# Head norms' sums of squares in two split passes, with the opening's loads and the store of x reordered

## The reference

```python
mod = silu(c) @ w_ada + b_ada                       # shift1, scale1, gate1, shift2, scale2, gate2
h = rms_norm(x, norm1_w) * (1 + scale1) + shift1
q_a, k_a, v_a, q_f, k_f, v_f, f_logit, g_a, g_f = split(h @ w_in)
q_a, k_a = rope(rms_norm(q_a, swa_q_norm_w)), rope(rms_norm(k_a, swa_k_norm_w))   # per head of 128
q_f, k_f = rms_norm(q_f, fox_q_norm_w), rms_norm(k_f, fox_k_norm_w)               # per head of 128
merged = sigmoid(g_a) * (window_attention @ w_o_swa) + sigmoid(g_f) * (forgetting_attention @ w_o_fox)
x = x + gate1 * (merged @ w_out)
x = x + gate2 * (silu(g) * u) @ w_ffn_out           # g, u from a second adaLN norm of x
```

## Time and profile before

| | |
|---|---|
| median of 3 runs | 2699.12 us (2698.11 to 2699.68) |
| profiled execution, its own time | 2696.75 us |
| span of the profiled execution | 2695.1 us |
| TensorE busy | 2637.9 us, 98% of the span |
| VectorE busy | 1970.2 us, 73% |
| ScalarE busy | 1034.2 us, 38% |
| mean transfer rate | 181 GB/s |

### The profile page before, as it was taken

One profiled execution on the slowest core, in us unless ns is written; L12 is line 12 of the kernel. 1 busy time (PEld: TensorE's weight loads), 2 busy tenths in 40 slices (PEclk: granted clock), 3 DMA queues, 4 the chain that ended last, 5 costly groups with the idle time before them and its releaser, 6 DMA issues.

```text
span 2695.1 us, 44512 instructions
## 1 busy us (share of the span) xinstructions
PE 2637.9 (98%) x17066; PEld 2397.4 (89%) x17066; DVE 1970.2 (73%) x3066; ACT 1034.2 (38%) x1402; POOL 298.8 (11%) x290
## 2 busy tenths in 40 slices
PE   5899999999999999999999999999999999999999
PEld 5678888878888888888899999999999999999998
DVE  6888877743333357755568888888888888888886
ACT  4332333333433322222354444444444444333343
POOL 0033223210001011122100000000000000010100
PEclk8999999999999999999999999999999999999999
DMA  9986666533333277777434444544544559595753
GB/s 334 294 256 181 179 187 173 148 100 94 102 94 102 71 226 242 235 233 233 151 94 157 158 136 157 160 137 154 163 136 151 165 203 339 166 347 177 262 214 120
DMA packets 399485, 487.17 MB, mean 181 GB/s; under 512 B 19029, under 2 KB 338793, under 8 KB 398793
## 3 DMA queue, kind: packets, MB, share of 16 engines
q1 hardware_dynamic: 364296, 353.12, 42.1%
q0 software_dynamic: 32896, 127.28, 13.5%
q10 hardware_dynamic: 2112, 4.19, 0.4%
HBM read 414.80 MB, written 69.73 MB: 180 GB/s over the span
## 4 chain that ended last, share of the span: by engine, by line
PE 91%; DMA 4%; DVE 2%; SPq 1%; issue 1%; ACT 1%; DVEq 0%; POOL 0%; ACTq 0%; POOLq 0%
PE bank L913 15%; PE bank L916 15%; PE bank L915 15%; PE bank L592 12%; PE bank L594 12%; PE bank L593 12%; DMA ramp_w<-in_w_ada 3%; PE bank L743 1%; PE bank L721 1%; PE bank L768 1%; SPq L482 1%; PE bank L732 1%; PE bank L862 1%; PE bank L866 1%; PE bank L864 1%
## 5 line engine op out<-in xcount | busy, mean ns | idle before, releaser
L913 PE MATMUL bank<-mov,w_slot 128*128 128x256 f32 x3472 | 983.6, 283 | 0.9 <-ACT blocks L1201 0.9
L916 PE MATMUL bank<-mov,w_slot 128*128 128x256 f32 x3472 | 982.6, 283 | 0.0
L915 PE MATMUL bank<-mov,w_slot 128*128 128x256 f32 x3472 | 982.5, 283 | 0.0
L913 PEld LDWEIGHTS bank<-mov,w_slot 128*128 128x128 f32 x3472 | 666.5, 192 | 1.1 <-ACT blocks L1201 1.1
L915 PEld LDWEIGHTS bank<-mov,w_slot 128*128 128x128 f32 x3472 | 666.6, 192 | 0.0
L916 PEld LDWEIGHTS bank<-mov,w_slot 128*128 128x128 f32 x3472 | 666.5, 192 | 0.0
L1289 DVE TENSOR_TENSOR w_lo<-w_raw,w_hi 128x1024 fp32r<-128x1024 f32 x192 | 241.8, 1260 | 377.7 <-ACT w_hi L943 377.0
L592 PE MATMUL bank<-h_hi,w_hi 128*128 128x512 f32 x1280 | 509.4, 398 | 0.0
L594 PE MATMUL bank<-h_hi,w_lo 128*128 128x512 f32 x1280 | 499.3, 390 | 0.0
L593 PE MATMUL bank<-h_lo,w_hi 128*128 128x512 f32 x1280 | 498.4, 389 | 0.0
L1140 ACT ACTIVATE w_slot<-w_raw 128x768 fp32r<-128x768 f32 x248 | 209.8, 846 | 557.7 <-PE bank L916 553.1
(11 more groups left out here) (241 smaller groups left out, 2784.1 us busy)
## 6 DMA issues: line engine op xcount, KB each, us to landing
w_raw<-in_w_ffn_in SPq DMA_DIRECT2D x352, 256.0 KB, 3.1
w_raw<-in_w_ada SPq DMA_DIRECT2D x128, 512.0 KB
w_raw<-in_w_ffn_out SPq DMA_DIRECT2D x88, 512.0 KB, 5.7
u_fm<-u_stage POOLq DMA_DIRECT2D x22, 1792.0 KB, 8.4
mov<-u_fm POOLq DMA_DIRECT2D x22, 1792.0 KB, 21.3
ramp_w<-in_w_ada SPq DMA_DIRECT2D x64, 512.0 KB, 8.8
w_raw<-in_w_in SPq DMA_DIRECT2D x128, 256.0 KB
w_raw<-in_w_in SPq DMA_DIRECT2D x64, 512.0 KB
```

Of the source, the lines that this page charges most:

```text
L913: nc.tensor.matmul(dst, lhsT=wh, rhs=xh, start=s == 0 and t == 0, stop=False, skip_group_check=True)
L915: nc.tensor.matmul(dst, lhsT=wh, rhs=xl, start=False, stop=False, skip_group_check=True)
L916: mm = nc.tensor.matmul(dst, lhsT=wl, rhs=xh, start=False, stop=last, skip_group_check=True)
```

## The change

The squares of a head tile are cut into high and low part as well, and summed over partitions in two fp32r passes with a matrix of ones of that type. ScalarE squares each tile a second time into an fp32r tile (in space of `val` and `rot` that is not in use then), VectorE subtracts it from the first square, and TensorE waits for that. Transfers of the opening move: eight small loads, `fl_raw` and the five tables from SyncE's queue to ScalarE's; the wait ahead of the head stage's loads becomes one for the first four products of the last w_ada block; x is stored in 16 transfers, two in each head. VectorE takes half of the copies of the transposed x.

```diff
+        def sum_squares(dst, hi, low):
+            nc.tensor.matmul(dst, lhsT=ones_r[:], rhs=hi, start=True, stop=False)
+            return nc.tensor.matmul(dst, lhsT=ones_r[:], rhs=low, start=False, stop=True)
...
             load_x(0)
             load_x(1)
-            sp.wait_ge(vec_zeroed, 1)
...
             load_x(2)
             load_x(3)
             for j in range(STEP):
                 load_quarter(0, j)
-            sp.dma_start(fl_raw[:].rearrange("p (k n) -> p k n", k=KD), w_in_k[:, :, FL0:FL0 + HQ]).then_inc(fl_landed, 16)
...
-            sp.wait_ge(ramp_mod, 2 * G_N)
...
+            summed(2 * STEP * (G_N - 1) + 1)
...
                 pe.wait_ge(y_stats, y + 1)
-                nc.tensor.matmul(bank[6][:], lhsT=ones[:], rhs=tile(sq, 0), start=True, stop=True)
+                pe.wait_ge(y_sq_low, y + 1)
+                sum_squares(bank[6][:], y_sq_hi(y), tile(sq_low, 0))
...
+                        pe.wait_ge(x_sq_low, i + 1)
                         for t in range(2):
-                            mm = nc.tensor.matmul(bank[4 + t][:], lhsT=ones[:], rhs=tile(sq, t),
-                                                  start=True, stop=True)
+                            mm = sum_squares(bank[4 + t][:], x_sq_hi(i, t), tile(sq_low, t))
...
+            act.wait_ge(vec_zeroed, 1)
...
             act.wait_ge(vecs_copied, 1)
...
-                for q in range(4):
+                for q in range(2):
                     act.wait_ge(x_turned, 4 * tb + q + 1)
...
                 nc.scalar.activation(tile(sq, 0), bank[b][:], ACT.Square)
+                nc.scalar.activation(y_sq_hi(y), bank[b][:], ACT.Square).then_inc(y_squared, 1)
...
+            act.wait_ge(ramp_mod, 2 * G_N)
...
...
             def heads(i, last):
                 for j in range(A_N):
                     split(ph_a, i, j, last)
+                    if j == 0:
+                        spill_x(i)
...
+                        for t in range(2):
+                            x_square = nc.scalar.activation(x_sq_hi(i, t), bank[2 + t][:], ACT.Square)
+                        x_square.then_inc(x_sq_done, 1)
...
+            for tb in range(TB):
+                for q in range(2, 4):
+                    dve.wait_ge(x_turned, 4 * tb + q + 1)
+                    v.tensor_copy(x_raw[:].rearrange("p (k n) -> p k n", k=KD)[:, 4 * q:4 * q + 4, tb * P:(tb + 1) * P],
+                                  bank[q][:].rearrange("p (k n) -> p k n", k=4)).then_inc(xt_dve, 1)
             dve.wait_ge(cact_done, 1)
...
+            def y_low(y):
+                dve.wait_ge(y_squared, y + 1)
+                v.tensor_tensor(tile(sq_low, 0), tile(sq, 0), y_sq_hi(y).bitcast(F32), ALU.subtract
+                                ).then_inc(y_sq_low, 1)
+            def x_low(i):
+                dve.wait_ge(x_sq_done, i + 1)
+                for t in range(2):
+                    low = v.tensor_tensor(tile(sq_low, t), tile(sq, t), x_sq_hi(i, t).bitcast(F32), ALU.subtract)
+                low.then_inc(x_sq_low, 1)
             for j in range(LEAD):
                 split(ph_a, 0, j - LEAD, False)
+                if j == 0:
+                    y_low(0)
...
             y_norm(0)
...
             def heads(i, last):
+                y_low(i + 1)
                 for j in range(A_N):
                     split(ph_a, i, j, last)
                     if j == 1:
                         y_norm(i + 1)
+                    if j == 4:
+                        x_low(i)
```

More of the change, by code:

```diff
@@ L207, in build_block @@
             o += cols
-        assert SMALL + 4 * o <= FORGET
+        assert SMALL + 4 * o <= ONES
         ident, ones, mod, bada, vec = (small[n] for n in ("ident", "ones", "mod", "bada", "vec"))
         cact, a1, a2, wy, wx = (small[n] for n in ("cact", "a1", "a2", "wy", "wx"))
-        sinks, sel, bf, eps, ss, rr = (small[n] for n in ("sinks", "sel", "bf", "eps", "ss", "rr"))
+        sinks, sel, bf, eps = (small[n] for n in ("sinks", "sel", "bf", "eps"))
         colraw, rowmax, negmax, rowsum = (small[n] for n in ("colraw", "rowmax", "negmax", "rowsum"))
+        ss, rr = rowmax, negmax
         esink, rinv, sinkcol = (small[n] for n in ("esink", "rinv", "sinkcol"))
@@ L352, in numbers, with y_sq_hi, x_sq_hi @@
             return ph["r"] + ph["n"] * i + j, u % RING, u // RING + i * (k * ph["n"] // RING)
+        def y_sq_hi(y):
+            return tile(val_r, y)
+        def x_sq_hi(i, t):
+            return tile((rot_r, val_r)[t], i + KVH)
+        def sum_squares(dst, hi, low):
+            nc.tensor.matmul(dst, lhsT=ones_r[:], rhs=hi, start=True, stop=False)
+            return nc.tensor.matmul(dst, lhsT=ones_r[:], rhs=low, start=False, stop=True)
         def each(eng, n, body, start=0):
@@ L615, in _ @@
                 for q in range(4):
-                    n = 4 * tb + q
-                    if n >= 4:
-                        pe.wait_ge(xt_copied, n - 3)
+                    if tb:
+                        pe.wait_ge(xt_copied if q < 2 else xt_dve, 2 * tb + q % 2 - 1)
                     for k in range(4 * q, 4 * q + 4):
@@ L948, in copy_cols @@
                 nc.scalar.activation(colraw[:], bank[4][:, 0:2], ACT.Copy).then_inc(col_copied, 1)
+            act.wait_ge(vec_zeroed, 1)
+            for v, r0 in ((c, 0), (norm1_w, KD), (norm2_w, 2 * KD)):
+                act.dma_start(vecrows[r0:r0 + KD, 0:P], v.rearrange("a (r p) -> (a r) p", p=P)).then_inc(vec_landed, 16)
+            for n, w in enumerate((swa_q_norm_w, swa_k_norm_w, fox_q_norm_w, fox_k_norm_w)):
+                act.dma_start(vecrows[3 * KD + n:3 * KD + n + 1, 0:P], w).then_inc(vec_landed, 16)
+            act.dma_start(vecrows[0:6 * KD, P:2 * P], b_ada.rearrange("a (r p) -> (a r) p", p=P)).then_inc(vec_landed, 16)
+            act.dma_start(fl_raw[:].rearrange("p (k n) -> p k n", k=KD), w_in_k[:, :, FL0:FL0 + HQ]).then_inc(fl_landed, 16)
             act.wait_ge(vecs_copied, 1)
@@ L1013, in y_roots, with spill_x @@
                 nc.scalar.activation(tile(val, y), bank[7][:], ACT.Copy).then_inc(y_stats, 1)
[L1015 to L1019, removed]
+            def spill_x(i):
+                for k in (i, i + KD // 2):
+                    act.dma_start(x_fm[bass.ds(k, 1)].rearrange("k p s -> p (k s)"), tile(x_raw, k)).then_inc(x_spilled, 16)
+            act.wait_ge(ramp_mod, 2 * G_N)
+            act.dma_start(cos[:], consts[:, P:P + S]).then_inc(tab_landed, 16)
+            act.dma_start(sin[:], consts[:, P + S:P + 2 * S]).then_inc(tab_landed, 16)
+            act.dma_start(sel[:], consts[:, CONST_W - HQ:CONST_W]).then_inc(tab_landed, 16)
+            act.dma_start(sinks[:], swa_sinks.to_broadcast([P, HQ])).then_inc(tab_landed, 16)
+            act.dma_start(bf[0:HQ, :], b_forget.rearrange("a h -> h a")).then_inc(tab_landed, 16)
             act.wait_ge(unit_done, G_N - 1)
@@ L1316, in _ @@
             v.memset(ones[:], 1.0).then_inc(ones_set, 1)
+            dve.wait_ge(ones_set, 1)
+            v.tensor_copy(ones_r[:], ones[:])
             v.memset(fq_rows[:].bitcast(F32), 0.0)
@@ L1433, in _ @@
             each(dve, A_I, heads)
+            y_low(KVH + HQ - 1)
             y_norm(KVH + HQ - 1)
```

38 lines of the change are left out of this document (20 added, 18 removed).

## The result

The changed kernel takes 2685.18 us (median of 6 runs, 2684.14 to 2687.21), the kernel before 2699.44 us on the same chip (6 runs, 2698.11 to 2700.21): a ratio of 0.995, with a 95% interval of 0.994 to 0.996. It is 14.3 us faster; the forecast of 2699.1 us said no change, and its range ended at 2692. The profiled execution took 2687.01 us, 9.7 us less than that of before.

The account below looks back on a forecast made before the run. TensorE, holding 91% of the chain, was taken as the bound, with the opening bound by bytes. Opening -1.5, head 0 +4.8, remaining sums -8.9, later heads +5.6 gave 0.0: 2699.1 us, own range 2692.8 to 2704.1, 2692 to 2705.5 without A and C.

Parts of the forecast that it names:

- Part 1: Sums of squares on TensorE: two fp32r passes 0.23 us apart replace one fp32 sum, 0.405 us saved each, 26 sums, 10.5 us.
- Part 2: Later heads: TensorE waits for x_low's subtractions, GpSimd taking a turn between; 0.8 us lost in each of seven heads, +5.6 us.
- rival B: Only later heads' waits are small: x_low wins the port, 0.3 us a head, opening gives 3; 2692.8 us, chance 0.15.
- Part 3: Head 0: new 5.9 us wait at y_post(1), x_post(0) at 185.3 against 179.69 us; net +4.8 us, bounds +3.5 and +6.0.
- The clock: Head 0, after the wait at x_post(0): TensorE's slow clock costs the same 1.8 us as before, no difference.
- Part 5: Opening: small loads leave SyncE's queue for ScalarE's, easing the transfer sag at 20 to 30 us; -1.5 us, bounds -3.0 and +0.5.
- The prediction's own sign of being wrong: Among the signs listed as showing the forecast wrong: the opening's end moved by more than 3 us.
- the hole that was to be filled: Transfers at 124 GB/s before the head stage: loads begun some 14 us earlier fill it, changing nothing TensorE awaits before unit 3.
- My upper bound of +0.5 us: Opening: the slower bound, if VectorE's eight copies of x, now ahead of its first products, delay it.
- Part 6: Store of x in 16 transfers of 256 KB, two a head, beside 8 MB of weights: costs nothing.
- the prefetch: Head 0: early loads cannot help, as from unit 3 on VectorE paces this stage and not the transfers.

Follow-up runs that it names:

- the run alone: The kernel before with only FORGET, and so w_slot2, moved up by 352 bytes: 2688.76 against 2698.62 us, ratio 0.9964.
- the run with y_low first: The changed kernel with the second head's subtraction y_low(1) put ahead of the reciprocal y_norm(0): 2683.62 us, ratio 0.9943.

## Why the prediction was wrong

**The step that failed is the one that is missing.** The sum held every instruction that the change adds, and nothing for what the new buffer did to the addresses. The diff shows that FORGET moves, and the kernel that w_slot2 lies there. I gave it no term, no bound and no rival, and the argument that a part whose code is untouched keeps its time was never written down, only used. It measured -8.9 us by the pitch and -9.9 by the run alone, more than every term but the sums. Rows of before could have raised the question: passes of 256 columns start exactly 120 ns apart in the feed-forward part and passes of 512 columns 227 in the projections, so 256 more columns cost 107 ns, and 13 ns of each pass are for something else. They could not have answered it, as no row of before has another distance.

**Part 1, the price of a pass: right.** Two fp32r passes start 0.23 us apart (282.68, 282.92) and the period fell by 1.25 us in a head with no wait, against 3 x 0.405 forecast.

**Part 2, later heads: the term was mis-sized.** 0.8 us a head were forecast for the turn that GpSimd would take between the subtractions, and nothing came in six heads, 0.72 us in the last: 5.6 became 0.7, which is 4.9 us of the difference. From x1 to y9 stand 14 x sums and 6 y sums, 20 x 0.405 = 8.1 us; 307.15 became 299.80, 7.35 less, and the last head's wait is the rest. Two things differ from the forecast. GpSimd did not come between: it is issued 0.16 us after the first subtraction and ends at 282.65, so that its own 0.74 us began near 281.9, about when the second subtraction ended. And VectorE's products began 3.50 us ahead of TensorE's sums (279.18 to 282.68), where I had reckoned with 2.70 (273.65 to 276.35); 0.33 of that was a transfer's lateness in the head that I had read the earlier trace rows. The Trainium skill, "SBUF — State Buffer", section "SBUF: two separate sides", says that whichever of the two starts first holds the port for its whole instruction; the trace agrees as to the first subtraction, and adds that a second one that follows without a gap (281.37) passed the waiting GpSimd too, while beside the long rotations the turns alternate. I took the rows of the rotations for the rule of all pairs. This is rival B's mechanism, which had a chance of 0.15. B's time of 2692.8 us was wrongly added up, though: with head 0 at +4.8, as B left it, it is 2694.1. That the kernel without the address gain stands at 2693.8 is in part luck, as B's 3 us in the opening did not come.

**Part 3, head 0: right in its mechanism.** The wait of 5.9 us at y_post(1) measured 5.51, and y0 to x0 was to be 41.3 us (144.0 to 185.3) and measured 40.8 (the sum to 179.5 in it makes 179.6, which changes nothing); that VectorE's chain paces the head is what the run with y_low first shows. The clock was worth less than I said: x0 to x1 took 47.82 us, where the sums' saving alone would give 48.2, so the slow stretch behind the wait still costs, but 0.4 us less. TensorE stood still for 3.21 us and not for 5.65. The granted clock is 0.50 from 188 to 191 us and 0.81 in the next, and the first passes are 0.43 us apart (189.46, 189.89): the lower of its two levels.

**Part 5, the opening: the gain did not come.** Its start of y_post(0) was to come 1.5 us earlier, less 0.5 for the new square. In eight profiled executions with the old opening y_post(0) starts at 143.5 to 145.5 us, mean 144.7; in five with the new one at 144.1 to 147.7, mean 145.6 (the sums alone, with the old opening and the new square, have 145.6 too). The means differ by less than the scatter, so only the forecast gain is refuted, and a loss is not shown. The prediction's own sign of being wrong, an opening's end moved by more than 3 us, stands in the two profiles (143.49 to 147.68) and is for the most part this scatter. The sag of transfers between 20 and 30 us went as forecast, but TensorE's gain from it did not come, and the hole that was to be filled only moved. My upper bound of +0.5 us, VectorE's copies ahead of its products, is the nearer end. The scatter of 2 to 4 us was in none of my bounds. It goes in part with the granted clock of the first 143 us (0.92 in the earliest, 0.84 in the latest, but 0.90 and 0.87 at 145.2 and 144.1); the profiled execution of before was 1.2 us early in it, the one of after 2.1 late. That would make 3.3 of the 4.6 us by which the medians' difference (14.3) exceeds the profiles' (9.7).

**Part 6 and the prefetch: not nothing.** With fp32 sums, the new store and the earlier loads shortened head 0 by 4.0 us (36.20 + 49.42 to 33.89 + 47.72). ScalarE's timeline shows where, in the rounding that stands ahead of x's eviction. Before, it waits for a transfer:
```profile
176.39 1.06 ACT L943 ACTIVATE w_hi<-w_raw 128x1024 fp32r<-128x1024 f32 x1 [3.69 <-DMA w_raw<-in_w_in]
```
and in the kernel with fp32 sums, whose y0 was 2.0 us later, for TensorE's unit alone:
```profile
176.12 1.06 ACT L949 ACTIVATE w_hi<-w_raw 128x1024 fp32r<-128x1024 f32 x1 [4.98 <-PE bank L600]
```
Whether the store in parts or the early loads do it, no run separates. I had said that VectorE and not the transfers paces this stage; true of the changed kernel, where part of this gain is hidden behind the new waits.

**The sum again, as measured.** Address -8.9; heads from y0 to y9 -4.4 instead of about +1; opening about +0.9 in the mean; the rest, a microsecond or two, lies within the scatter. Without the address the kernel stood at 2693.8, inside the forecast's range of 2692 to 2705.5 but 5.3 below its number.

## What to carry to other kernels

A change that adds or enlarges a buffer moves every buffer behind it, so list what moved and look at the pitch of the passes that read it, even in stages whose code is the same: here 352 bytes shifted a third of the passes by 2%. Where TensorE is the bound, is never idle and has a full clock, compare start-to-start times of one form between kernels, not its busy share, and try the weights' offset as a parameter, for each stage by itself: 64 bytes, 192 in one slot, were worth 66 us here, and cost 27 in another stage. Where TensorE waits at the end of an engine's long chain, count what stands ahead of that instruction: a subtraction put earlier only moved the wait (5.5 us gone, 7.1 more at the next), and 2.7 us of work taken out from in front shortened it by 2.8, of which the time showed little.

## What was not expected of the hardware

TensorE's pitch depends on where its weights lie relative to what moved with the other operand: 120.0, 118.3 and 113.6 ns with the weights moved by 0, 32 and 64 bytes for passes of 256 columns, and in the opposite sense, 227 and 233 ns, for the projections' 512 columns. Clock and idle time show nothing of it. The Trainium skill, "SBUF — State Buffer", section "SBUF: two separate sides", says that TensorE's access waits for no other engine; these runs do not contradict it, as the other engines do the same work in the fast kernels, and it does not speak of a cost that follows the distance alone. What makes the two stages want different distances is the form of the pass, and not the stage, the slot's length or how often it is rewritten. With slot 2 alone moved by 352 bytes, its passes of 512 columns in the first sixteen feed-forward units start 234 ns apart (median) for 227, while its passes of 256 columns in those same units have a mean of 118.4 ns for 120, and in the later units 117.45. Why the form matters stays open. Slot 2 at one and the same address had 117.45 ns with the other slots in place and 118.7 with them moved as well, which stays open too.
